# Queries projected transposed, with the rotary turn split between GpSimd, a DMA and VectorE, in a two-layer hybrid decoder

## The reference

```python
h = rms_norm(x, norm_mix_pre[i])
proj = h @ w_in[i]
a_u, a_v, b_q, b_k, b_v, b_g, c_q, c_k, c_v = split_cols(proj, IN_SIZES)   # 256 256 384 384 384 384 384 128 128
y_a = gmlp_mixer(a_u, a_v, ...)
y_b = retention_mixer(b_q, b_k, b_v, b_g, ret_gn_w[i])
y_c = swa_sink_mixer(c_q, c_k, c_v, attn_sinks[i])
mix = jnp.concatenate([y_a, y_b, y_c], axis=-1) @ w_out[i]
x = x + rms_norm(mix, norm_mix_post[i])
```

## Time and profile before

| | |
|---|---|
| median of 3 runs | 1225.6 us (1225.6 to 1225.62) |
| the profiled execution | 1225.42 us, its span 1223.7 us |
| PE busy | 1217.0 us (99% of the span), 7873 instructions |
| DVE, ACT, POOL busy | 841.5 (69%), 616.0 (50%), 136.6 us (11%) |
| chain that ended last | PE 98%, DVE 1% |
| PE's waits | 2.8 us in total, the longest 1.2 us |
| granted PE clock | full in all 40 slices |

### The profile page before, as it was taken

The page is one execution under the profiler, slowest core; times in us unless marked ns, Lnnn a source line. Parts: engine busy times, 40 slices in busy tenths (PEclk is TensorE's granted clock), DMA queues, the critical chain, the costliest instruction groups (busy, mean ns, idle before and its releaser), DMA issues.

```text
span 1223.7 us, 20397 instructions
## 1 busy us (share of the span) xinstructions
PE 1217.0 (99%) x7873; PEld 1109.8 (91%) x7873; DVE 841.5 (69%) x1365; ACT 616.0 (50%) x1204; POOL 136.6 (11%) x208
## 2 busy tenths in 40 slices
PE   9999999999999999999999999999999999999998
PEld 8988888999999988888899889889999999888887
DVE  5685646888888853267976756468988887433788
ACT  7454435555555532237664544364655555422474
POOL 2003621100000000003030037020000000000120
PEclk9999999999999999999999999999999999999999
DMA  7322232233333354320242222231333333444001
GB/s 247 111 65 91 70 103 69 70 104 104 104 105 106 109 183 154 124 67 18 86 119 73 91 75 90 74 103 53 104 105 106 108 101 119 163 147 172 18 18 70
DMA packets 124464, 122.31 MB, mean 100 GB/s; under 512 B 5200, under 2 KB 108752, under 8 KB 124368
## 3 DMA queue, kind: packets, MB, share of 16 engines
q1 hardware_dynamic: 123680, 120.48, 31.4%
q10 hardware_dynamic: 688, 0.53, 0.2%
HBM read 118.90 MB, written 2.10 MB: 99 GB/s over the span
## 4 chain that ended last, share of the span: by engine, by line
PE 98%; DVE 1%; ACT 0%; POOL 0%; issue 0%; DVEq 0%; ACTq 0%
PE bank L1004 31%; PE bank L1006 30%; PE bank L1005 30%; PE bank L1214 2%; PE bank L1273 1%; PE bank L1294 1%; PE bank L1333 1%; PE bank L1317 1%; PE bank L1309 0%; PE bank L1281 0%; PE bank L1329 0%; PE bank L1338 0%; PE bank L1224 0%; PE bank L1359 0%; PE bank L1255 0%; DVE ple_n L2196 0%
## 5 line engine op out<-in xcount | busy, mean ns | idle before, releaser
L1004 PE MATMUL bank<-w_hi,h_hi 128*128 128x384 f32 (+2 forms) x564 | 200.4, 355 | 0.8 <-DVE w_lo L1893 0.7
L1005 PE MATMUL bank<-w_lo,h_hi 128*128 128x384 f32 (+2 forms) x564 | 194.6, 345 | 0.0
L1891 DVE TENSOR_TENSOR w_lo<-raw,w_hi 128x1024 fp32r<-128x1024 f32 x70 | 83.6, 1233 | 133.7 <-ACT w_hi L1411 133.5
L1004 PE MATMUL bank<-h_hi,w_hi 128*128 128x256 f32 x568 | 161.0, 284 | 0.1
L1006 PE MATMUL bank<-h_hi,w_lo 128*128 128x256 f32 x568 | 160.7, 283 | 0.0
L1005 PE MATMUL bank<-h_lo,w_hi 128*128 128x256 f32 x568 | 160.7, 283 | 0.0
L1006 PE MATMUL bank<-w_hi,h_lo 128*128 128x384 f32 (+2 forms) x468 | 157.5, 336 | 0.0
L1411 ACT ACTIVATE w_hi<-raw 128x1024 fp32r<-128x1024 f32 x70 | 70.6, 1053 | 160.7 <-PE bank L1006 160.6
L1006 PE MATMUL bank<-w_hi,mid_lo 128*128 128x512 f32 x352 | 137.0, 389 | 0.0
L1004 PE MATMUL bank<-T_hi,w_hi 128*128 128x256 f32 x448 | 126.8, 283 | 0.0
L1005 PE MATMUL bank<-T_lo,w_hi 128*128 128x256 f32 x448 | 126.8, 283 | 0.0
(11 more groups left out here) (294 smaller groups left out, 2909.3 us busy)
## 6 DMA issues: line engine op xcount, KB each, us to landing
raw<-in_w_ffn_in SPq DMA_DIRECT2D x88, 512.0 KB, 3.9
raw<-in_w_ffn_out SPq DMA_DIRECT2D x44, 512.0 KB, 4.2
raw<-in_w_in SPq DMA_DIRECT2D x40, 384.0 KB, 3.8
raw<-in_w_out SPq DMA_DIRECT2D x16, 512.0 KB, 3.8
gw<-in_w_gate SPq DMA_DIRECT2D x16, 512.0 KB, 3.4
raw<-in_w_in SPq DMA_DIRECT2D x10, 512.0 KB, 4.6
raw<-in_w_ple SPq DMA_DIRECT2D x4, 512.0 KB, 5.9
x<-in_x_in SPq DMA_DIRECT2D x3, 512.0 KB, 6.9
```

The source lines that it names most:

```text
L1004: pe.matmul(out_ap, a_hi, b_hi, start=start, stop=False, skip_group_check=True)
L1005: pe.matmul(out_ap, a_hi, b_lo, start=False, stop=False, skip_group_check=True)
L1891: last = dve.tensor_tensor(lo, raw[q % RAWS][:, cols], hi, ALU.subtract)
```

## The change

The columns of `w_in` are put in another order on the host: cq and bq stand side by side, cq's heads in pairs. These 768 columns are three groups of 256, qa, qb, qc, one strip each. `mm_turned` uses 128 weight columns as the weights in the array and moves all 512 tokens: a block is 2 units (k-slices 0 to 3 and 4 to 7), its result has the query's dimensions on partitions, in bank i % 4. Blocks 0 to 2 are cq, 3 to 5 bq, so no query is transposed any more; the strips number 12 for 13 and the units 4 to 47. In layer 1 block 0 is computed for 384 tokens ahead of ckv m = 3 (`q_most`), and for the last 128 behind it.

The rotation of a block: ACT copies the bank to `q_raw` and issues four DMAs on its own queue that bring the halves of each head, exchanged, to `q_turn` (8 or 32 partitions each); POOL multiplies `q_raw` by a table of cosines into `cT` or `qT`; DVE multiplies `q_turn` by signed sines and adds. The tables (4 of 128x512) are loaded by SP in each layer ahead of strips 3 and 4; POOL fills `q_turn` with zeros. `r_mix` no longer scales cq; it goes into the maximum's factor and into the exponentials' scale (`s_qn`, `s_q`, two small POOL products per tile). bk stays as it was. `ret_T` transposes bk alone, `swa_T` is one event with ck's four transposes. The hand-made unit numbers change:

```diff
 GROUPS = {
     "ckv": (2 * AW + 5 * BW, 256),
-    "cq": (2 * AW + 4 * BW, BW),
-    "bk": (2 * AW + BW, BW),
-    "bq": (2 * AW, BW),
-    "bv": (2 * AW + 2 * BW, BW),
+    "qa": (2 * AW + 3 * BW, 2 * P),
+    "qb": (2 * AW + 3 * BW + 2 * P, 2 * P),
+    "qc": (2 * AW + 3 * BW + 4 * P, 2 * P),
+    "bk": (2 * AW, BW),
+    "bv": (2 * AW + BW, BW),
...
+    for i in range(2 * len(TURNED)):
+        put(6 + 2 * i, "q_rope", i)
+    put(8, "swa_T")
     for c in range(TILES):
-        put(10 + c, "swa_T", c)
-        u = (13, 18, 23, 28)[c]
+        u = (12, 16, 21, 26)[c]
         put(u, "swa_cur", c)
         if c:
             put(u + (1 if c < 3 else 2), "swa_yhi", c - 1)
         put(u + 1, "swa_prev", c)
         if c:
             put(u + (1 if c < 2 else 2), "swa_ylo", c - 1)
-        put(u + (2, 1, 2, 2)[c], "swa_norm", c)
-        put(u + 5, "swa_PT", c)
-        put(u + (5, 5, 3, 5)[c], "swa_mask", c)
-        put(u + 7, "swa_o", c)
+        put(u + (2, 2, 2, 1)[c], "swa_norm", c)
+        put(u + (4 if c == 0 else 5), "swa_PT", c)
+        put(u + (4 if c == 0 else 5), "swa_mask", c)
+        put(u + (6 if c == 0 else 7), "swa_o", c)
...
-        u = (33, 37, 41, 45)[c]
+        u = (30, 34, 38, 42)[c]
         for step, name in zip((0, 2, 3), ("ret_T", "ret_sc", "ret_o")):
             put(u + step, name, c)
-        put(41 + c, "gmlp_v", c)
-        put(42 + c, "gmlp_n", c)
+        put(37 + c, "gmlp_v", c)
+        put(38 + c, "gmlp_n", c)
     for c in range(TILES):
-        put(48 + c, "ret_norm", c)
-        put(50 + c, "ret_yT", c)
+        put(44 + c, "ret_norm", c)
+        put(46 + c, "ret_yT", c)
...
             mm(ins[0], 2, nxt)
+            add("q_most", lay=nxt)
+            mm(ins[0], 3, nxt)
             mm(ins[1], 0, nxt)
             mm(ins[1], 1, nxt)
-            mm(ins[0], 3, nxt)
...
+                if 3 <= s < 5:
+                    i = s - 3
+                    if layer:
+                        sp.wait_ge(g_mm, g_count(layer - 1, 4))
+                        sp.wait_ge(x_new, x_count(layer - 1, "gate", 3))
+                    sp.dma_start(cos_q[i][:], turns[2 * i]).then_inc(turns_loaded[i], 16)
+                    sp.dma_start(sin_q[i][:], turns[2 * i + 1]).then_inc(turns_loaded[i], 16)
...
+            def mm_turned(layer, i, half, cols):
...
+                pe.wait_ge(h_lo_ready, h_count(layer, "mix", (cols.stop - 1) // P, half))
+                pe.wait_ge(lo_ready, 2 * g + 1 + half)
...
+                for k in range(4 * half, 4 * half + 4):
+                    last = mm3(banks[i % 4][:, cols], hi[:, k, c], lo[:, k, c], h_hi[:, k, cols], h_lo[:, k, cols],
+                               k == 0, k == KD - 1)
...
+                        act.wait_ge(mm_done, mm_count(layer, strip, m))
+                        if n > 2:
+                            act.wait_ge(q_roped, n - 2)
...
+                        act.activation(q_raw[b][:], banks[i % 4][:, :], ACT.Copy).then_inc(q_evac, 1)
+                        act.wait_ge(q_evac, n)
+                        half = HD // 8 if i < 3 else HD // 2
+                        for r in (0, HD):
+                            for d in (r, r + half):
+                                src = 2 * r + half - d
+                                act.dma_start(q_turn[b][d:d + half, :],
+                                              q_raw[b][src:src + half, :]).then_inc(q_turned[b], 16)
...
+                    pool.tensor_tensor((cT, qT)[which][:, i % 3, :], q_raw[i % 2][:], cos_q[which][:],
+                                       ALU.mult).then_inc(q_cos, 1)
...
+                    dve.wait_ge(q_turned[b], 64 * (3 * layer + i // 2 + 1))
+                    step(dve.tensor_tensor(q_turn[b][:], q_turn[b][:], sin_q[which][:], ALU.mult))
+                    dve.wait_ge(q_cos, n)
+                    done(dve.tensor_tensor(dst, dst, q_turn[b][:], ALU.add), q_roped)
```

More of the change, by code:

```diff
@@ L200, in plan_schedule @@
         mm(o[0], 0)
-        for u in (52, 53):
-            if u == 53:
+        for u in (48, 49):
+            if u == 49:
                 mm(o[1], 0)
@@ L388, in small_tables @@
     table = np.concatenate([np.eye(P), rc, rs, sc, ss, lower_t, qs, ks], 1)
-    return np.ascontiguousarray(table.astype(f)), later
+    turns = np.zeros((4, P, S), f)
+    for i, (half, theta) in enumerate(((HD // 8, 500000.0), (HD // 2, 10000.0))):
+        inv = (1.0 / (f(theta) ** (np.arange(half, dtype=f) / f(half)))).astype(f)
+        a = (pos[None, :] * inv[:, None]).astype(f)
+        turns[2 * i] = 1.0
+        for r in (0, HD):
+            turns[2 * i, r:r + half] = turns[2 * i, r + half:r + 2 * half] = np.cos(a).astype(f)
+            turns[2 * i + 1, r:r + half] = -np.sin(a).astype(f)
+            turns[2 * i + 1, r + half:r + 2 * half] = np.sin(a).astype(f)
+    return np.ascontiguousarray(table.astype(f)), later, turns
 TABLE_COLS = {}
@@ L402, in build_trunk @@
                 post_mix, pre_ffn, w_ffn_in, w_ffn_out, post_ffn, w_gate, w_ple, ple_norm,
-                table, later, out):
+                table, later, turns, out):
     KB = 1024
@@ L519, in build_trunk @@
     r_mix = [small(1) for _ in range(TILES)]
+    s_q = [small(1) for _ in range(TILES)]
+    s_qn = [small(1) for _ in range(TILES)]
     nsnk = small(C_HEADS)
@@ L579, in build_trunk @@
     ck_roped = sem("ck_roped")
-    cq_roped = sem("cq_roped")
+    turns_loaded = [sem(f"turns_loaded{i}") for i in range(2)]
+    q_evac = sem("q_evac")
+    q_turned = [sem(f"q_turned{i}") for i in range(2)]
+    q_roped = sem("q_roped")
+    q_scaled = sem("q_scaled")
+    q_cos = sem("q_cos")
+    q_zeroed = sem("q_zeroed")
     b_roped = sem("b_roped")
@@ L1017, in mm_in @@
                     gi = GNAMES.index(name)
-                    if gi:
+                    if name == "bk":
+                        pe.wait_ge(q_evac, 6 * layer + (5, 6, 3, 4)[m])
+                    elif gi:
                         pe.wait_ge(*evac(layer, GNAMES[gi - 1], m))
@@ L1161, in block_of @@
                     pe.wait_ge(lo_ready, 2 * (g + 1))
-                if kind == "in":
+                if kind == "in" and strip[1] in TURNED:
+                    block = 2 * TURNED.index(strip[1]) + m // 2
+                    last = mm_turned(layer, block, m % 2, slice(S - P if layer and block == 0 else 0, S))
+                elif kind == "in":
                     last = mm_in(layer, g, strip, m)
@@ L1313, in _ @@
                     c = e[1]
-                    pe.wait_ge(ret_kqT, layer * TILES + c + 1)
+                    pe.wait_ge(ret_kT, layer * TILES + c + 1)
+                    if c == 0:
+                        pe.wait_ge(q_roped, 6 * layer + 6)
                     for j in range(3):
                         for g in range(2):
-                            last = pe.matmul(banks[4 + g][:, j * P:(j + 1) * P], kqT[rows(g), 0, j, :],
-                                             kqT[rows(g), 1, j, :], start=True, stop=True,
+                            last = pe.matmul(banks[4 + g][:, j * P:(j + 1) * P], kT[rows(g), j, :],
+                                             qT[rows(g), j, ts(c)], start=True, stop=True,
                                              skip_group_check=True)
@@ L1699, in _ @@
                     act.wait_ge(ret_T, layer * TILES + c + 1)
[L1700 to L1704 removed]
+                    act.activation(kT[:], banks[4][:, 0:BW].rearrange("p (k t) -> p k t", k=3),
+                                   ACT.Copy).then_inc(ret_kT, 1)
                 elif kind == "ret_o":
@@ L2363, in _, with turned_last @@
                         dve.wait_ge(mm_done, mm_count(layer, strip, m))
-                        rope_full(layer, DVE_EVAC.index(name), m)
+                        rope_full(m)
+def turned_last(w):
+    a, bq, bk, bv, bg, cq, ckv = np.split(w, np.cumsum([2 * AW] + 5 * [BW]), 2)
+    cq = cq.reshape(*w.shape[:2], C_KV, C_HEADS // C_KV, HD).transpose(0, 1, 3, 2, 4).reshape(cq.shape)
+    return np.concatenate([a, bk, bv, bg, cq, bq, ckv], 2)
 def heads_in_pairs(w):
@@ L2385 @@
     depth = w_in.shape[0]
-    table, later = small_tables()
+    table, later, turns = small_tables()
     values = {
@@ L2396 @@
         "w_gate": w_ple_gate, "w_ple": w_ple_proj, "ple_norm": ple_norm,
-        "table": table, "later": later,
+        "table": table, "later": later, "turns": turns,
     }
```

132 lines of the change are left out of this document (77 added, 55 removed).

## The result

The kernel after takes **1256.6 us** (median of four runs, 1253.9 to 1258.4) against 1225.6: ratio 1.0252, 95% interval 1.0229 to 1.0274. Forecast were 1233.6 us and a range up to 1238.5. The direction was right; the size was not: the loss is 31 us and not 8.

The account below looks back on a forecast made before the run. TensorE, busy 99% of the span, was taken as the bound, by what it issues and by results that reach it late. 1225.4 - 5.0 (PE's work) + 1.0 (layer boundary) + 12.2 (three late results) = 1233.6 us; range 1224.0 to 1238.5.

Parts of the forecast that it names:

- PE's own work: What PE issues in both layers: mainly fewer transposes, 48 in all; -5.0 us in all.
- layer boundary: Start of layer 1: the second strip's longer conv delays DVE's split of token tile 2; +1.0 us, once.
- (a): y_lo of chunk 2, for which the first ret_T waits at unit 30: late by 2.2 us a layer.
- (b): ACT's copy of chunk 2's own-key scores, awaited by its previous-key scores at unit 22: late by 2.3 us a layer.
- (c): scm of chunk 2, for which the third ret_o waits at unit 41: late by 1.6 us a layer.
- Late by 2.2 us; PE's queue moves as a whole, so it is lost: At the first ret_T, unit 30: y_lo of chunk 2 comes 2.2 us late, and that time is lost.
- Together 2.2 + 2.3 + 1.6 = 6.1 a layer: The three late results (a), (b) and (c) added up: 6.1 us a layer, +12.2 us.
- The slack of 8.1 against 6.1 at chunk 0: From block 2's end to chunk 0's scores: 8.1 us available for a rotation chain of 6.1, so no wait.
- the transfers or ACT's issues were sized too small: Sign to look for in the profile after: what a wait at chunk 0's scores would say.
- rival 4: More waits than counted: POOL's products holding DVE back at chunk 0's norm, 1235.8 us, or slower landings, 1237 to 1240; chance 0.12.
- 1 to 3: Rivals: nothing late, 1221.4 us (0.13); only (a) real, 1225.8 (0.1); (a) and one other, 1229.0 to 1230.4 (0.2).

Follow-up runs that it names:

- e14: The order of e9 with the rotation of the queries left out; 1223.15 us.
- e1: The kernel after, with ten 512-column matmuls of zeros ahead of each of TensorE's three long waits, in both layers; 1248.0 us.
- e15: The kernel before, with twelve equal stalls of TensorE of 2.64 us in the second feed-forward product; 1277.5 us.
- e12: The kernel after with its own order, the rotation of the queries left out; 1248.5 us.
- e8: The kernel after, with two of the four transfers of each block left out, so ScalarE issues two; 1248.7 us.
- e7: The kernel after, with the queries' product with the cosines on VectorE and not on GpSimd; 1255.8 us.
- e2: The kernel after, with chunk 3's norm a unit later in VectorE's queue; 1255.6 us.
- e17: The kernel of e9 with the conv of the next layer's second strip behind the split of token tile 2; 1230.1 us.
- e9: The kernel after with three late results moved up, then the whole retention and the gated group's variance one unit later; 1231.4 us.
- e16: The kernel of e9 with the boundary's conv moved and two of each block's four transfers issued by GpSimd, not ScalarE; 1227.3 us.

## Why the prediction was wrong, step by step

The profiled execution is 32.8 us above its like of before (1258.2 - 1225.4), the forecast sum 8.2. By its terms:

| term | forecast | measured |
|---|---|---|
| PE's own work | -5.0 | -4.2 (e14) |
| layer boundary | +1.0 | +0.8 |
| (a) y_lo 2 | 2 x 2.2 | 2 x 2.76 |
| (b) copy of chunk 2's scores | 2 x 2.3 | 2 x 2.62 |
| (c) scm 2 | 2 x 1.6 | 2 x 2.5 |
| chunk 0 and the second scores of chunk 1 | 0 | 2.4 and 3.7 |
| half clock behind the waits | no term | 13.6 (12.6 by e1) |
| sum | 8.2 | 32.1 |

- **The step that failed** is "Late by 2.2 us; PE's queue moves as a whole, so it is lost", and with it "Together 2.2 + 2.3 + 1.6 = 6.1 a layer": it prices a late result at the time that PE waits. The runs showed the wait and a stretch at half clock behind it. 13.6 of the 24.6 us missed are this. It was not in the sum, the rivals or the range, since in the kernel before PE never waits longer than 1.2 us and its clock never falls: the profile of before could not price it, and I took the cost of the unseen as nothing instead of naming it. Shown by e1 (the waits kept, the clock full, 8.6 us less) and by e15 (2.64 us of waiting costs 4.4). It is not the only one: at full clock e1 still takes 1248.0 us, above the range's 1238.5. Of the other 11.0 us, 6.1 are the waits at chunk 0 and chunk 1's second scores, which the forecast put at nothing, 3.6 are (a) to (c), 0.6 are PE's own work and the boundary together, and 0.7 no term here holds.
- **PE's own work** was right in kind and 0.8 too good.
- **The layer boundary** was right: its conv took 3.25 (634.17), as in the earlier trace rows, and the wait was 0.83.
- **(a), (b), (c)** were at the right places, (a) and (c) for the right reasons, and 0.3 to 0.9 each too small, 3.6 us over both layers. In (a), ACT's six exponentials take 0.48 each from start to start (103.03 and 103.51) and not the 0.41 of the earlier trace rows; their scale is now a column of numbers (`s_q`) and not a constant. I had that line of the diff as "it goes into the maximum's factor and into the exponentials' scale" and gave it nothing. The six take 0.45 longer, most of the 0.56 by which (a) was short. The Trainium skill ("ScalarE: Activation LUTs", section "What ACT_TABLE_LOAD costs") states a price for just this, about 93 ns for each operand that is a pointer to a column instead of an immediate; the trace agrees, the median of 48 exponentials is 0.481 us where it was 0.388 before. In (c) the conv of the out strip took 3.01 (150.34) where I had 2.4 "by like shapes". POOL's chain was 7.7, as in the earlier trace rows. That (a) and (c) owe nothing to the turning is shown by e12, which keeps the packing and the scale. In (b) the size came near for a wrong reason: 1.6 of its 2.3 was to be DVE's late start by block 5's work, and e12, without that work, still waits 1.95.
- **The slack of 8.1 against 6.1 at chunk 0** failed. Block 2 ends at 39.6, and the scores were due at 47.7, 8.1 later, as reckoned. But its copy began at 41.25, 1.6 us behind its end and not 0.2, since ACT had a conv and the copy of ck's transposes first; the issues took 2.6 us (41.86) and not 1.9, the data were there 2.3 after the last (46.81), the two DVE operations took 1.9 and not 1.4. With the 0.6 of the copy that is 9.0, and the wait of 1.03. Chunk 0's transposes then wait for a chain which has a mask of 2.17 beside POOL and ACT's issues in it, and in layer 1 the table load of 1.28. e8 shows that the issues carry most of it. The forecast named this as a sign ("the transfers or ACT's issues were sized too small"), but gave it a chance of only 0.12, within rival 4.
- **Rivals.** 1 to 3 are refuted. Rival 4, more waits than counted, was right in kind, and its 1235.8 to 1240 still short. The wait that it placed at chunk 0's norm by contention did not come there: POOL's product of block 5 began behind the norm, which took 0.96 (60.08), and POOL's was the one drawn out. It came at the mask, 2.17 for 1.06, and e7 without it gains nothing.

The spread of the kernel after, 4.5 us over four runs where before has 0.2, is the clock's as well: the runs of 1258.4 and 1253.9 us have a mean granted clock of 0.988 and 0.993.

**What stays open** is why some waits of one length are followed by half clock and others are not. Over all traces here, of 66 waits of 2.4 us or more 57 were, of 19 between 1.4 and 2.3 five, of 49 between 0.6 and 1.1 none (e1's six filled waits and each kernel's start left out). More than the length must count (2.64 and 2.69 in layer 1 of e2, 2.70 in e17 went free). The slow stretches do not all begin where the wait ends, either: 0.87 us behind it at 82.54, 0.64 behind it at 154.45, at once at 110.75. So it may be what stands around a wait, or the moment at which it falls; no run varied one of them alone. Nor was it tried to have SP issue the transfers.

## What to carry to other kernels

Where PE is the bound and hardly waits, a change that packs its queue closer has to be priced with the late result, with the next result that comes late once that one is mended, and with the clock: here most waits of 2.4 us or more cost 1.4 to 3.4 us on top, and none up to 1.1 us did. A layer's first exponential can carry a table load besides. So take several short waits sooner than one long one (e9: 8.7 us of waits, none above 1.5, and no slow stretch behind any), or fill a long one with matmuls that add zeros, and look at the granted clock in windows of a few us, not in the page's slices. Of work moved to another engine, count also its DMA issues and operands that turn from a constant into a tensor; both stand in the queue of the engine that must answer PE next.

## What the hardware did that I had not expected

- The granted clock halves behind single waits of 2 to 4 us in a kernel that otherwise keeps PE at 98% or more, and comes back by itself; the loss is mostly 1.5 to 1.7 us, at times 2.5 to 3.4. Ten matmuls of zeros in the gap prevented it in all six places.
- A DMA issue costs ACT 0.63 us (median of 48, 0.51 to 1.38), as much as its copy of a 128x512 bank (0.58, 41.25); on POOL 0.52 (median of 24, e16), and there the transfer lands 2.8 us behind the issue (median).
- An exponential of 128x128 on ACT takes 0.48 us with a per-partition scale and 0.39 with a constant one (medians of 48, after and before), 0.48 and 0.41 from start to start.
- A load of ACT's function table, 1.28 us, stands ahead of the first exponential of layer 1 in the kernel before and the kernel after; only in the one after does it delay PE.
